# Order of work at the norms of a two-layer hybrid decoder step: first two projections chunk by chunk together, mean squares and roots placed elsewhere

## The chip, the cores and the metric

The kernel runs on one core of a Trainium2 chip. The metric is the device time of one execution in microseconds (us), here the median of three runs. Time is also given inside the profiled execution: its span is the time from the first to the last instruction, and all positions such as "at 38.41" are microseconds from the start of that span.

## The reference, cut to what matters

The program is one step of a small decoder with two layers, for 1024 prompt tokens and 8 sample tokens, 1032 tokens with 1024 features each, in float32. Layer 0 has a mixer of retention and gated delta net heads, layer 1 one of Mamba-2 heads; after each mixer comes a SwiGLU block. Around them stand five RMS norms:

```
def rmsnorm(x, w):
    xf = x.astype(jnp.float32)
    y = xf * lax.rsqrt(jnp.mean(xf * xf, axis=-1, keepdims=True) + EPS)
    return (y * w.astype(jnp.float32)).astype(x.dtype)

for i in range(DEPTH):                       # DEPTH = 2
    h = rmsnorm(x, norm_mix_w[i])
    out, ... = hybrid_mixer(h, ...) if i % 2 == 0 else ssm_mixer(h, ...)
    x = x + out
    x = x + swiglu(rmsnorm(x, norm_ffn_w[i]), ...)
y = rmsnorm(x, norm_final_w)
```

In the kernel they are numbered: norm 0 stands before the mixer of layer 0, norm 1 before its SwiGLU, norm 2 before the mixer of layer 1, norm 3 before its SwiGLU, norm 4 at the end. The states that the mixers also return are left out here, since the change doesn't touch them.

## The kernel before

**Layout.** `x` is kept transposed: 128 partitions hold the features of one of KC = 8 chunks (index c), the free dimension holds the T = 1032 tokens, cut into TG = 3 groups of TN = 344 (index g). TensorE multiplies in a float32 format with fewer bits, so each operand is split into a high and a low part (`h_hi`, `h_lo`, `w_hi`, `w_lo`), and each product is three matmuls: high by high, low by high, high by low. In `group_products` (line 569) that is for one chunk and one group, 128x128 weights against 344 columns.

**Weights** come as units of 128x1024 (all eight chunks of one output tile). SP loads a unit into one of two slots of `w_raw`, GpSimd makes `w_hi` (line 492) and `w_lo` (line 495) of it and counts `w_split` up. GpSimd starts on unit u only when `unit_done` says that TensorE has finished unit u - 2, and SP reloads a slot of `w_raw` when it has been split.

**The results** of projections go to two sets of PSUM banks, `ps_set[0]` and `ps_set[1]`. Jobs take them in turn: `take` waits until whoever read the job before the last in the same set has counted it free. Small results, the mean squares among them, go in the same way to `ps_core[0]` and `ps_core[1]`.

**A norm** is called a boundary; each engine has a function `boundary(n, ...)` that writes out its own order, and the engines meet by semaphores with named steps. There is no planner: program order on each engine is all.

- ScalarE `squares(g)`: two squares of four chunks each (128x1376). For group g it waits until the sum of group g - 1 is made, since they share a buffer.
- VectorE `sums(g)`: two additions (lines 1697 and 1699) that leave 128x688.
- TensorE `mean_square(g)` (line 585): four recorded matmuls with a matrix of ones.
- ScalarE `root(g)`: Ln from `ps_core`, then Exp with -0.5. Each of the two has a table load in front of it.
- VectorE `scaled(g)`: for each chunk one multiplication h = x * weight * root (line 1718) into one of three rotating buffers `h_block`; ScalarE `highs(g)` copies it to `h_hi`; VectorE's `low` (line 1704) makes `h_lo`. Low c - 2 comes behind h c, and h c waits for low c - 3.
- TensorE `projections(g)`: the first two projections of the next stage (`first`: q and k at norm 0, the first gate and up tiles at norms 1 and 3, the scalars and x0 at norm 2), for group g, each chunk waiting for `lo{c}.{g}`. All chunks of the first projection come before those of the second.

Norms 0, 2 and 4 go this way. At norms 1 and 3 the root is not multiplied into h: ScalarE writes `h_hi` as x times the weight (`products`), VectorE `h_lo` (`lows`, line 1729), and the root of all three groups (`logs`, then one Exp) is used behind the projections. So there TensorE need not wait for mean squares, only whoever reads the root.

In front of norms 1, 2 and 3 stand the last outputs of the stage before (`outputs_of(g)`, also line 574 by the record), which VectorE adds to `x` (`add(g, q)`: line 1780 in norms 1, 2 and 4, lines 1811 and 1815 in norm 3). Norm 0 has no outputs: `x` comes by DMA from SP, group by group, and ScalarE's `later_constants` issues four DMAs behind its first squares.

The orders before, g standing for the group:

- TensorE, norms 1 and 3: outputs 0, 1, 2; projections 0; mean square 0; projections 1; mean square 1; projections 2 with mean square 2 between its two.
- TensorE, norms 0, 2, 4: outputs 0, 1; mean square 0; outputs 2; mean square 1; projections 0; mean square 2; projections 1; projections 2.
- ScalarE, norms 0, 2, 4: squares 0, squares 1, root 0, squares 2, highs 0, root 1, highs 1, root 2, highs 2.
- VectorE, norms 0, 2, 4: adds mixed with sums 0 and sums 1, scaled 0, sums 2, scaled 1, scaled 2.

Of the kernel before, what the change touches and what calls it, by code (L numbers as in the profile page):

```python
# [24 lines left out]
KC = D // P  # L25
NP_TOK, ND_TOK = 1024, 8
T = NP_TOK + ND_TOK
TG = 3
# [151 lines left out]
def build(nc, a, o, book):  # L180

    ctx = ExitStack()
    with ctx:
# [364 lines left out]
        def _(pe):  # L548
# [29 lines left out]
            def boundary(n, outputs_of, first):  # L578
# [9 lines left out]

                def projections(g, between=lambda: None):
                    for k, (jobs, job, unit) in enumerate(first):  # L590
                        if k:
                            between()
                        if g == 0:
                            take(jobs, job)
                            pe.wait_ge(w_split, unit + 1)
                        for c in range(KC):
                            pe.wait_ge(*norm_dve[n].value(f"lo{c}.{g}"))
                            mm = group_products(ps_set[jobs.part(job)][:, g, :], unit % 2, c, (h_hi[:, c, :], h_lo[:, c, :]), g,
                                                c == 0, c == KC - 1)
                        if g == TG - 1:  # L600
                            mm.then_inc(unit_done, 1)

                if n in (1, 3):
                    for g in range(TG):
                        outputs_of(g)
                    projections(0)
                    mean_square(0)
                    projections(1)
                    mean_square(1)
                    projections(2, lambda: mean_square(2))  # L610
# [5 lines left out]
                mean_square(1)  # L616
                projections(0)
                mean_square(2)
                projections(1)
# [509 lines left out]
        def _(act):  # L1129
# [20 lines left out]
            def boundary(n):  # L1150
# [29 lines left out]
                def highs(g):  # L1180
                    for c in range(KC if n < 4 else 0):
# [28 lines left out]
                if n == 0:  # L1210
                    later_constants()
                    act.wait_ge(consts_in, 48)
                squares(1)
                root(0)
                squares(2)
                highs(0)
                root(1)
                highs(1)
                root(2)
# [469 lines left out]
        def _(dve):  # L1689
            v = nc.vector  # L1690

            def boundary(n, add):
# [14 lines left out]
                def scaled(g):  # L1707
                    dve.wait_ge(*norm_act[n].value(f"rstd{g}"))
                    for c in range(KC):
# [12 lines left out]
                    if n < 4:  # L1722
# [38 lines left out]
                if n == 0:  # L1761
                    dve.wait_ge(consts_in, 48)
                adds(0, 0)
# [6 lines left out]
                adds(2, 1)  # L1770
                scaled(0)
                sums(2)
                scaled(1)
# [812 lines left out]
```

## Time and profile before

| | |
|---|---|
| median of 3 runs | 3323.36 us (3321.98 to 3327.50) |
| span of the profiled execution | 3317.2 us |
| mean granted TensorE clock | 0.986 |
| TensorE busy | 3143.7 us, 95% |
| VectorE busy | 1775.8 us, 54% |
| GpSimd busy | 1019.1 us, 31% |
| ScalarE busy | 799.8 us, 24% |

The profiled execution has no time of its own beside its span; the three runs stand 4.8 to 10.3 us above the span, which holds only what lies between the first and the last instruction. In the rows below PE is TensorE, PEld its weight loads, DVE VectorE, ACT ScalarE, POOL GpSimd, SP SyncE. A helper records all of ScalarE's operations as line 1131, so there the tiles tell which is which: `work<-ps_core,small` is Ln, `work<-work` of 128x344 is Exp, `work<-x` a square, `h_hi<-work` a high part. The stretches of the norms in the span are: norm 0 from 0 to 62, norm 1 from 885 to 934, norm 2 from 1648 to 1709, norm 3 from 2478 to 2567, norm 4 from 3276 to the end.

### The profile page before, as it was taken

The page shows a single profiled execution, that of the slowest core. Times are in us where ns is not written, and L with a number is a line of the kernel's source. Part 1 is how long each engine was busy: PE and PEld are TensorE (multiplying, and loading weights), DVE is VectorE, ACT ScalarE, POOL GpSimd, SP SyncE. Part 2 cuts the span into 40 slices and gives each one's busy share as a digit, 9 for nine tenths or more (in the row PEclk, how much of TensorE's full clock was granted, in tenths as well). Part 3 has the DMA queues.
Part 4 walks back from the last instruction along what each step waited for, and adds up shares of the span by engine and source line. Part 5 has one row for each costly group of instructions (what it writes and reads, how often), then busy time and mean ns, then how long its engine had stood idle before and what let it go on. Part 6 is the DMA issues. An engine that isn't in the chain of part 4 may idle for free. (4 is left out here: it accounts for less than half of the span.)

```text
span 3317.2 us, 46817 instructions
## 1 busy us (share of the span) xinstructions
PE 3143.7 (95%) x20090; PEld 3030.1 (91%) x20090; DVE 1775.8 (54%) x2023; ACT 799.8 (24%) x1176; POOL 1019.1 (31%) x528
## 2 busy tenths in 40 slices
PE   6999899998899999999989998999988999999997
PEld 5899898888799999999988897989978999999997
DVE  5344657566543333333487869678696333333335
ACT  4222414324420000000145415243253000000002
POOL 2222201111023333333334536345362333333331
PEclk9999999999899999999999999999999999999999
DMA  4111100101011111111113214132231111111111
GB/s 147 59 71 59 49 26 33 40 26 40 21 44 45 50 46 45 45 51 45 45 42 121 86 58 148 62 118 74 82 128 37 51 45 45 50 47 45 46 51 64
DMA packets 94474, 198.15 MB, mean 60 GB/s; under 512 B 21796, under 2 KB 52164, under 8 KB 94152
## 3 DMA queue, kind: packets, MB, share of 16 engines
q1 hardware_dynamic: 52384, 150.03, 12.9%
q10 hardware_dynamic: 41896, 45.23, 4.3%
q8 instruction: 159, 2.61, 0.3%
q14 instruction: 35, 0.29, 0.0%
HBM read 171.41 MB, written 19.59 MB: 58 GB/s over the span
## 5 line engine op out<-in xcount | busy, mean ns | idle before, releaser
L492 POOL CAST w_hi<-w_raw 128x1024 fp32r<-128x1024 f32 x230 | 256.8, 1116 | 2181.2 <-PE ps_set L565 1971.5
L565 PE MATMUL ps_set<-h_hi,w_hi 128*128 128x344 f32 x3648 | 806.0, 329 | 2.2 <-DVE work L2179 1.3
L565 PE MATMUL ps_set<-h_lo,w_hi 128*128 128x344 f32 x3648 | 776.8, 321 | 0.0
L565 PE MATMUL ps_set<-h_hi,w_lo 128*128 128x344 f32 x3648 | 772.0, 320 | 0.0
L565 PEld LDWEIGHTS ps_set<-h_hi,w_hi 128*128 128x128 f32 x3648 | 615.5, 189 | 26.8 <-issue 18.7
L565 PEld LDWEIGHTS ps_set<-h_lo,w_hi 128*128 128x128 f32 x3648 | 619.9, 190 | 0.0
L565 PEld LDWEIGHTS ps_set<-h_hi,w_lo 128*128 128x128 f32 x3648 | 610.6, 188 | 0.0
L495 POOL TENSOR_TENSOR w_lo<-w_raw,w_hi 128x1024 fp32r<-128x1024 f32 x230 | 599.0, 2605 | 18.4
L1824 DVE TENSOR_TENSOR x<-x,ps_set 128x1032 f32<-128x1032 f32 x160 | 196.7, 1229 | 255.6 <-PE ps_set L565 255.6
L1131 ACT ACTIVATE work<-work 128x1032 f32<-128x1032 f32 (+5 forms) x190 | 180.7, 959 | 496.0 <-DVE work L2179 447.9
L565 PE MATMUL ps_set<-y_hi,w_hi 128*128 128x344 f32 x1296 | 282.7, 327 | 8.5 <-DVE y_lo L2360 7.0
L1131 ACT ACTIVATE y_hi<-work 128x1032 fp32r<-128x1032 f32 (+1 forms) x98 | 63.5, 662 | 882.9 <-PE ps_set L565 633.3
L565 PE MATMUL ps_set<-y_lo,w_hi 128*128 128x344 f32 x1296 | 274.6, 320 | 0.0
L565 PE MATMUL ps_set<-y_hi,w_lo 128*128 128x344 f32 x1296 | 273.9, 319 | 0.0
L2179 DVE TENSOR_TENSOR work<-work,ps_set 128x1032 f32<-128x1032 f32 x44 | 54.1, 1229 | 340.4 <-PE ps_set L565 324.0
L565 PEld LDWEIGHTS ps_set<-y_hi,w_hi 128*128 128x128 f32 x1296 | 216.0, 189 | 13.4 <-issue 11.3
L565 PEld LDWEIGHTS ps_set<-y_lo,w_hi 128*128 128x128 f32 x1296 | 218.0, 189 | 0.0
L565 PEld LDWEIGHTS ps_set<-y_hi,w_lo 128*128 128x128 f32 x1296 | 216.5, 189 | 0.0
L836 PEld LDWEIGHTS ps_core<-work 128*128 128x128 f32 x1344 | 159.0, 194 | 29.0 <-issue 8.8
L836 PE MATMUL ps_core<-work 128*128 128x128 f32 x1344 | 169.0, 283 | 16.9 <-DVE work L2071 7.9
L1131 ACT ACTIVATE work<-ps_core 128x512 f32<-128x512 f32 (+3 forms) x164 | 72.9, 451 | 433.5 <-PE ps_core L836 140.2
L1131 ACT ACTIVATE work<-ps_set 128x1032 f32<-128x1032 f32 x72 | 74.3, 1032 | 289.1 <-PE ps_set L565 260.7
(229 smaller groups left out, 3652.7 us busy)
## 6 DMA issues: line engine op xcount, KB each, us to landing
w_raw<-in_w SPq DMA_DIRECT2D x230, 512.0 KB, 3.2
work<-ssm_cum_rows ACTq DMA_DIRECT2D x32, 512.0 KB, 4.8
sample<-in_ssm_state SPq DMA_DIRECT2D x16, 512.0 KB, 5.1
out_ssm_s<-sample SPq DMA_DIRECT2D x16, 512.0 KB, 2.8
x<-in_x SPq DMA_DIRECT2D x6, 688.0 KB, 15.5
work<-work ACTq DMA_DIRECT2D x16, 258.0 KB, 2.4
out_y<-x SPq DMA_DIRECT2D x6, 688.0 KB, 3.4
sample<-bc_rows SPq DMA_DIRECT2D x8, 512.0 KB, 4.7
```

The lines of the kernel that those rows point to most:

```text
L492: return nc.gpsimd.tensor_copy(w_hi[:, k, :], w_raw[:, k, :])
L495: return nc.gpsimd.tensor_tensor(w_lo[:, k, :], w_raw[:, k, :], w_hi[:, k, :].bitcast(F32), ALU.subtract)
L565: mm = nc.tensor.matmul(out[:, g, 0:TN], w[:, slot, cols], v[:, g * TN:(g + 1) * TN], start=(start and n == 0), stop=(stop and n == 2))
L836: mm = nc.tensor.matmul(ps_core[part][:, c * P:(c + 1) * P], blk(lhs)[:, 4 * hf + c], blk(rhs)[:, 4 * hf + c], start=True, stop=True)
L1131: return nc.scalar.activation(out, in_, func, **kw)
L1824: v.tensor_tensor(grp(x[:, t, :]), grp(x[:, t, :]), big(jobs.part(job)), ALU.add).then_inc(jobs.sem(job), 1)
L2179: v.tensor_tensor(grp(tok(c)), grp(RSTD), big(jobs.part(name)), ALU.mult).then_inc(jobs.sem(name), 1)
```

## The change

TensorE gets `together(g)`: for each chunk the products of both projections, one after the other, with a place for other work behind chunk 3. At group 0 it takes both PSUM sets and waits for both weight units ahead of the first product. At norms 1 and 3 it is used for groups 0 and 1; at norm 3 mean square 0 moves behind group 1's products, and mean squares 1 and 2 between the two projections of group 2. At norm 0 mean square 1 moves behind chunk 3 of group 0 and mean square 2 behind chunk 3 of group 1; at norm 2 mean square 2 moves behind chunk 3 of group 0. Group 2 keeps one projection after the other.

ScalarE and VectorE are reordered at norms 0 and 2 alone. At norm 0 root 0 comes ahead of squares 1, and squares, sums and roots of the later groups come in the middle of `highs` and `scaled` of the group before. At norm 2 squares 2 move ahead of most of highs 0, and roots 1 and 2 become Ln, Ln, Exp, Exp, between highs 5 and highs 6 of group 0. Norm 4 keeps its order on all engines.

```
--- before.py
+++ after.py
@@ -586,37 +586,60 @@
                                               start=(k == 0), stop=(k == 1))
                     mm.then_inc(*norm_pe[n].step(f"ms{g}"))
 
+                def product(jobs, job, unit, c, g):
+                    return group_products(ps_set[jobs.part(job)][:, g, :], unit % 2, c, (h_hi[:, c, :], h_lo[:, c, :]), g,
+                                          c == 0, c == KC - 1)
+
+                def together(g, between=lambda: None):
+
+                    if g == 0:
+                        for jobs, job, unit in first:
+                            take(jobs, job)
+                            pe.wait_ge(w_split, unit + 1)
+                    for c in range(KC if first else 0):
+                        pe.wait_ge(*norm_dve[n].value(f"lo{c}.{g}"))
+                        for jobs, job, unit in first:
+                            product(jobs, job, unit, c, g)
+                        if c == 3:
+                            between()
+                    if not first:
+                        between()
+
                 def projections(g, between=lambda: None):
                     for k, (jobs, job, unit) in enumerate(first):
                         if k:
                             between()
-                        if g == 0:
-                            take(jobs, job)
-                            pe.wait_ge(w_split, unit + 1)
                         for c in range(KC):
                             pe.wait_ge(*norm_dve[n].value(f"lo{c}.{g}"))
-                            mm = group_products(ps_set[jobs.part(job)][:, g, :], unit % 2, c, (h_hi[:, c, :], h_lo[:, c, :]), g,
-                                                c == 0, c == KC - 1)
-                        if g == TG - 1:
-                            mm.then_inc(unit_done, 1)
+                            mm = product(jobs, job, unit, c, g)
+                        mm.then_inc(unit_done, 1)
 
                 if n in (1, 3):
                     for g in range(TG):
                         outputs_of(g)
-                    projections(0)
-                    mean_square(0)
-                    projections(1)
-                    mean_square(1)
-                    projections(2, lambda: mean_square(2))
+                    together(0)
+                    if n == 1:
+                        mean_square(0)
+                    together(1)
+                    mean_square(1 if n == 1 else 0)
+
+                    def rest():
+                        if n == 3:
+                            mean_square(1)
+                        mean_square(2)
+                    projections(2, rest)
                     return
                 outputs_of(0)
                 outputs_of(1)
                 mean_square(0)
                 outputs_of(2)
-                mean_square(1)
-                projections(0)
-                mean_square(2)
-                projections(1)
+                if n == 2:
+                    mean_square(1)
+                    together(0, lambda: mean_square(2))
+                    together(1)
+                else:
+                    together(0, lambda: mean_square(1))
+                    together(1, lambda: mean_square(2))
                 projections(2)
 
             def pair_outputs(jobs, job, turn, slot, blocks, rhs, g, done):
@@ -1177,8 +1200,8 @@
                     fn(rstd_of(n, g), ps_core[core.part(f"ms{g}")][:, 0:TN], ACT.Ln, scale=1.0 / D, bias=EPS_C)\
                         .then_inc(core.sem(f"ms{g}"), 1)
 
-                def highs(g):
-                    for c in range(KC if n < 4 else 0):
+                def highs(g, first=0, last=KC):
+                    for c in range(first, last if n < 4 else 0):
                         act.wait_ge(*norm_dve[n].value(f"h{c}.{g}"))
                         fn(h_hi[:, c, span(g)], h_block(n, c), ACT.Copy).then_inc(*norm_act[n].step(f"hi{c}.{g}"))
 
@@ -1210,13 +1233,35 @@
                 if n == 0:
                     later_constants()
                     act.wait_ge(consts_in, 48)
+                    root(0)
+                    highs(0, 0, 4)
+                    squares(1)
+                    highs(0, 4, 6)
+                    root(1)
+                    highs(0, 6)
+                    highs(1, 0, 4)
+                    squares(2)
+                    highs(1, 4, 6)
+                    root(2)
+                    highs(1, 6)
+                    highs(2)
+                    return
                 squares(1)
                 root(0)
+                highs(0, 0, 2)
                 squares(2)
-                highs(0)
-                root(1)
+                if n == 4:
+                    root(1)
+                    root(2)
+                    return
+                highs(0, 2, 6)
+                logs(1)
+                logs(2)
+                for g in (1, 2):
+                    act.wait_ge(*core.read(f"ms{g}"))
+                    fn(rstd_of(n, g), rstd_of(n, g), ACT.Exp, scale=-0.5).then_inc(*norm_act[n].step(f"rstd{g}"))
+                highs(0, 6)
                 highs(1)
-                root(2)
                 highs(2)
 
             def scalars(layer, unit):
@@ -1704,9 +1749,10 @@
                     v.tensor_tensor(h_lo[:, c, span(g)], h_block(n, c), h_hi[:, c, span(g)].bitcast(F32), ALU.subtract)\
                         .then_inc(*norm_dve[n].step(f"lo{c}.{g}"))
 
-                def scaled(g):
-                    dve.wait_ge(*norm_act[n].value(f"rstd{g}"))
-                    for c in range(KC):
+                def scaled(g, first=0, last=KC):
+                    if first == 0:
+                        dve.wait_ge(*norm_act[n].value(f"rstd{g}"))
+                    for c in range(first, last):
                         if n == 4:
                             v.scalar_tensor_tensor(x[:, c, span(g)], x[:, c, span(g)], NORM_W[:, n, c:c + 1], rstd_of(n, g),
                                                    ALU.mult, ALU.mult).then_inc(*end_dve.step(f"y{g}.{c}"))
@@ -1719,7 +1765,7 @@
                                                ALU.mult, ALU.mult).then_inc(*norm_dve[n].step(f"h{c}.{g}"))
                         if c >= 2:
                             low(g, c - 2)
-                    if n < 4:
+                    if n < 4 and last == KC:
                         low(g, KC - 2)
                         low(g, KC - 1)
 
@@ -1759,7 +1805,16 @@
                     return
 
                 if n == 0:
+                    sums(0)
                     dve.wait_ge(consts_in, 48)
+                    scaled(0, 0, 4)
+                    sums(1)
+                    scaled(0, 4)
+                    scaled(1, 0, 4)
+                    sums(2)
+                    scaled(1, 4)
+                    scaled(2)
+                    return
                 adds(0, 0)
                 adds(0, 1)
                 adds(1, 0)
@@ -1767,9 +1822,19 @@
                 adds(1, 1)
                 adds(2, 0)
                 sums(1)
-                adds(2, 1)
-                scaled(0)
+                if n == 4:
+                    adds(2, 1)
+                    scaled(0)
+                    sums(2)
+                    scaled(1)
+                    scaled(2)
+                    return
+                add(2, 2)
+                scaled(0, 0, 2)
+                add(2, 3)
+                scaled(0, 2, 4)
                 sums(2)
+                scaled(0, 4)
                 scaled(1)
                 scaled(2)
```

## Rows read from the trace of the kernel before

**Rows 1.** The page: span and busy time of each engine.
```profile
span 3317.2 us, 46817 instructions
PE 3143.7 (95%) x20090; PEld 3030.1 (91%) x20090; DVE 1775.8 (54%) x2023; ACT 799.8 (24%) x1176; POOL 1019.1 (31%) x528
```
**Rows 2.** Stretches: length, busy by engine, granted clock, DMA share, GB/s.
```profile
0.00:62.00 62.00, 34.69 (x156) 27.10 (x156) 33.86 (x58) 32.43 (x44) 12.21 (x10) 1.00 0.46 162
...
1648.00:1709.00 61.00, 51.46 (x279) 45.40 (x280) 44.91 (x69) 34.51 (x47) 12.45 (x7) 0.94 0.08 26
```
**Rows 3.** Timeline of TensorE, norm 0: start, length, instruction, idle before.
```profile
16.03 2.63 PE L585 MATMUL ps_core<-work,square 128*128 128x344 f32 x4 [16.03 <-DVE work L1699]
```
**Rows 4.** Timeline of ScalarE, norm 0.
```profile
21.00 1.35 ACT L1131 ACTIVATE work<-x 128x1376 f32<-128x1376 f32 x1 [2.88 <-DMA x<-in_x]
22.36 1.28 ACT L1131 ACT_TABLE_LOAD   x1
23.66 0.55 ACT L1131 ACTIVATE work<-ps_core,small 128x344 f32<-128x344 f32 x1
...
25.52 0.49 ACT L1131 ACTIVATE work<-work 128x344 f32<-128x344 f32 x1
```
**Rows 5.** Timeline of VectorE, norm 0.
```profile
22.38 1.59 DVE L1697 TENSOR_TENSOR work<-work 128x1376 f32<-128x1376 f32 x1 [6.49 <-ACT work L1131]
24.01 0.87 DVE L1699 TENSOR_TENSOR work<-work 128x688 f32<-128x688 f32 x1
26.04 1.55 DVE L1718 SCALAR_TENSOR_TENSOR work<-x,small,work 128x344 f32<-128x344 f32 x3 [1.16 <-ACT work L1131]
...
38.41 1.55 DVE L1718 SCALAR_TENSOR_TENSOR work<-x,small,work 128x344 f32<-128x344 f32 x3 [0.53 <-ACT work L1131]
...
49.38 1.55 DVE L1718 SCALAR_TENSOR_TENSOR work<-x,small,work 128x344 f32<-128x344 f32 x3 [2.94 <-ACT work L1131]
...
56.04 1.36 DVE L1704 TENSOR_TENSOR h_lo<-work,h_hi 128x344 fp32r<-128x344 f32 x3
```
**Rows 6.** The chain of work that ended last, norm 3: start, length, work.
```profile
2557.37 3.77 PE ps_set L574 x24
2561.14 1.17 PE ps_core L585 x4
```
**Rows 7.** Stretches of TensorE alone: length, busy, granted clock, DMA share, GB/s.
```profile
909.80:915.10 5.30, 5.27 (x18) 0.50 0.27 99
2531.60:2533.90 2.30, 0.00 (x0) 1.00 0.49 167
2547.00:2550.40 3.40, 3.40 (x14) 0.51 0.00 0
```
**Rows 8.** Timeline of GpSimd, norm 1.
```profile
906.90 2.51 POOL L495 TENSOR_TENSOR w_lo<-w_raw,w_hi 128x1024 fp32r<-128x1024 f32 x1
```
**Rows 9.** Timeline of TensorE, norm 1.
```profile
907.33 0.39 PE L574 MATMUL ps_set<-h_hi,w_hi 128*128 128x344 f32 x1 [1.69 <-DVE h_lo L1729]
...
909.83 0.65 PE L574 MATMUL ps_set<-h_hi,w_hi 128*128 128x344 f32 x1 [1.79 <-DVE h_lo L1729]
```
**Rows 10.** Timeline of VectorE, norm 2.
```profile
1670.65 1.64 DVE L1780 TENSOR_TENSOR x<-x,ps_set 128x688 f32<-128x688 f32 x2
1672.21 3.20 DVE L1718 SCALAR_TENSOR_TENSOR work<-x,small,work 128x344 f32<-128x344 f32 x3
...
1684.83 1.55 DVE L1718 SCALAR_TENSOR_TENSOR work<-x,small,work 128x344 f32<-128x344 f32 x3 [0.53 <-ACT work L1131]
...
1702.46 1.37 DVE L1704 TENSOR_TENSOR h_lo<-work,h_hi 128x344 fp32r<-128x344 f32 x3
```
**Rows 11.** Timeline of GpSimd, norm 2.
```profile
1671.71 2.36 POOL L495 TENSOR_TENSOR w_lo<-w_raw,w_hi 128x1024 fp32r<-128x1024 f32 x1
```
**Rows 12.** Timeline of TensorE, norm 3.
```profile
2538.62 0.43 PE L574 MATMUL ps_set<-h_hi,w_hi 128*128 128x344 f32 x1 [0.64 <-DVE work L1811]
...
2545.73 1.48 PE L585 MATMUL ps_core<-work,square 128*128 128x344 f32 x4 [3.08 <-DVE work L1699]
```

## The prediction

> **What bounds the kernel now.** First the busy shares of the page: TensorE is busy 95% of the span, the next engine in line with work of its own 54% [rows 1]. Between the norms TensorE hardly stops, so the change can only move time inside the norms. The busy time by stretch comes next: in the first 62 us TensorE is busy 34.7, in the 61 us around norm 2 51.5 [rows 2]. These two are bound by the chain square, sum, mean square, root, scaled, high part, low part, which VectorE and ScalarE share. Norms 1 and 3 multiply before the root is known, and there TensorE sets the length but for a few waits. So I read the timelines of the four norms, engine by engine, and lay the new order out with the old durations: each engine takes its instructions in program order and starts one when its last input is there.
>
> The unit prices. A root is Ln 0.55, table load 1.28, Exp 0.49, 2.35 us with the gaps; its first load runs while it waits [rows 4]. Two squares are 2.70 [rows 4], the two sums 2.50 (22.38 to 24.88) [rows 5]. Scaling eight chunks takes 8.02 (49.38 to 57.40, the end of the last three low parts): h0 to h2 in 1.5, then 1.04 for each pair of scaled and low, 1.36 for the last three lows [rows 5]. TensorE does eight chunks of one projection for one group in 3.77 and a mean square in 1.17 [rows 6]; one chunk is 0.47, of both projections 0.94. At half rate a mean square is 2.63 [rows 3] and 18 matmuls take 5.3 us at a granted clock of 0.50, that is 1.2 GHz [rows 7]: 0.88 a chunk, 1.75 for both.
>
> **Norm 0: +8.0.** Removed: the root of group 0 no longer waits behind the squares of group 1, whose x lands at 21.00 [rows 4]. Its mean square ends at 18.66 [rows 3], so the root is there at 18.69 + 2.35 = 21.04 instead of 26.01: 5.0 us early. ScalarE's four loads of constants stay ahead of it and SP's queue is untouched. Added: squares and sums of the next group stand inside the scaling, and its mean square stands behind the products of chunk 3.
> - h0 to h3 and two low parts, 21.07 to 24.15; high 3 ends 24.2; squares of group 1 to 26.95, in which VectorE has nothing to do; sums to 29.45.
> - Only then h4, low 2 (30.4), h5, low 3 (31.5). TensorE has done chunks 0 and 1 from 23.1 and stands still; chunks 2 and 3 at half rate take it to 34.0, the mean square to 35.5 (36.6 if all at half rate).
> - Behind that mean square ScalarE has high 6 and 7 queued, and VectorE behind those low 6, low 7 and all of group 1. Root to 37.9, two high and low parts 1.5: group 1 starts at 39.5. Before it was 38.41 [rows 5]: the 5.0 us are gone and 1.1 lost.
> - Group 1 to group 2, the same loop: first four h and two lows 3.2, squares 2.7, sums 2.5, h4 to low 3 2.05, products 0.94 to 1.75, mean square 1.17 to 2.63, root 2.37, last two high and low 1.5: 16.4 to 18.7. Before: 49.38 - 38.41 = 10.97 [rows 5]. Loss 5.5 to 7.7; as TensorE stands still for 5 us between chunks 1 and 2, I take half rate for part of it, 6.9.
> - Group 2 and the tail (its chunk 7, then the second projection) are as before.
> Sum 1.1 + 6.9 = 8.0; bounds 6.6 (full rate as soon as possible) and 9.6 (half rate to the end of both waits, chunk 2 too). Nothing later hides it: the next projection follows at once.
>
> **Norm 1: +0.1.** Taking both projections at group 0 adds a wait for the second weights, which GpSimd splits after the last output: its low part ends at 909.41 [rows 8]. Queued behind that wait is all of TensorE. Today TensorE does one chunk at 907.33 and then waits until 909.83 anyway [rows 9]: VectorE's second low part is held while GpSimd works. New: start at 909.5 with 16 chunks to do, not 15 from 909.83: 0.47 - 0.33 = +0.1. After it no wait is left on TensorE in either order. Bounds: -1.0, if the half-rate stretch of 5.3 us becomes 3.4 as in norm 3 [rows 7]; +0.4, if it lasts a little longer.
>
> **Norm 2: +1.5.** Group 2's squares go ahead, and the roots of groups 1 and 2 are grouped, Ln, Ln, Exp, Exp: two table loads fewer (2.6 us). But group 1's root now comes only after group 2's mean square, and that stands behind chunk 3 of group 0.
> - From 1670.65 [rows 10] VectorE does add 2, h0, h1 (one of them held to the end of GpSimd's low part, 1674.07 [rows 11], at the latest 1675.0), add 3, h2, low 0, h3, low 1 to 1677.1. Adds read PSUM and took their normal 1.64 for two beside GpSimd's cast; three h beside its low part took 3.20, not 1.55 [rows 5, 10]. Squares of group 2 to 1676.1 (1678.6 if add 3 comes behind a held h1), sums to 1679.6 (1681.1).
> - Low 3 at 1681.6, chunk 3 to 1682.6, mean square to 1683.7; ScalarE's Ln, table, Exp, Exp to 1686.6, high 6 and 7, low 7 at 1688.1. Group 1 starts at 1688.15, before 1684.83 [rows 10]: +3.3.
> - Before, group 2 waited for its root: 1684.83 to the last low at 1703.83 [rows 10]. New, both roots are there: 8.02 + 0.05 + 8.02 = 16.1, end 1704.25: +0.4. With add 3 late 1.6 more, with chunks and mean square at half rate 2.0 more. Bounds +0.4 and +4.0; I take 1.5, nearer the first, since adds were not held in the rows.
>
> On table loads: the trace has one before Ln and one before Exp, each 1.28, with the ACTIVATE 0.02 behind [rows 4]. The Trainium skill (ScalarE: Activation LUTs, What ACT_TABLE_LOAD costs, and Table sets) puts a switch at about 2.66 us with its drain, and says that Ln then Exp needs one load. By the first norm 2 would save 5.3, not 2.6, and come out at -1.2; by the second grouping saves one load at most and norm 2 costs 1.3 more. The rows bear out neither.
>
> **Norm 3: +0.8.** Today the second projection starts at 2538.62, when VectorE has read the bank of output 3; the first, 3.77 us, is done in that wait [rows 6, 12]. Together both wait for 2538.6, and the 3.77 come behind it. Removed: the 3.08 us stop at the mean square of group 0 [rows 12], and the half-rate stretch after it (14 matmuls in 3.4 us [rows 7], 1.7 lost). New: 2538.6 + 6 x 3.77 + 3 x 1.17 = 2564.7 at full rate. But TensorE stands still from the last output at 2531.6 [rows 7] to 2538.6; a stop of 3.1 us brought half rate, so I add up to half of norm 1's 5.3: 2567.3. Before, these products ended at 2557.37 + 3.77 + 1.17 + 3.77 = 2566.1 [rows 6]. Bounds -1.4 and +1.2; by the clock I take +0.8. The final root keeps its place 3.8 us ahead of TensorE's end.
>
> **Norm 4 and the rest: 0.** Its splits are empty or joined. Alternating two banks every three matmuls, which these rows don't price: 0, with under 1 us in all as its bound, since weights are loaded before each matmul either way. The last group of each norm still goes one projection after the other, so weights are released as before.
>
> **Sum:** 8.0 + 0.1 + 1.5 + 0.8 = +10.4 us on the span of 3317.2 [rows 1]. The median of the runs is 3323.36, 6.2 more, which lies outside the first and last instruction and which the change leaves alone: 3323.36 + 10.4 = 3333.8.
>
> **Rivals.** A measurement of this kernel can tell about 0.2%, 6.6 us, from no change.
> - *The early start carries (not slower), 0.10.* If the root of group 1 were there when high 6 is due (32.1), norm 0 would run at VectorE's pace: 21.07, 8.02 for each group and 5.2 twice for squares and sums end the last low at 55.5, not 57.4: -1.9. With -1.0, +0.4 and -1.4 in the others -3.9: 3319.5; half of this case may pass 0.2%. It needs the mean square at 29.7. For it: x is landed and VectorE idle. Against: the sums end at 29.45 and chunk 2's low part at 30.4.
> - *The clock pays for it (within 0.2%), 0.15.* Full rate after all new stops: 6.6 - 1.0 + 0.4 - 1.4 = +4.6: 3328.0. Half rate after a stop of 3.1 us speaks against it [rows 7, 12].
> - *Half rate in every new gap (slower), 0.20.* 9.6 + 0.4 + 4.0 + 1.2 = +15.2: 3338.6. For it: the new stops are 4 to 7 us long.
> - *My sum, 0.55,* with a range of its own of 3329 to 3338.
> Faster 0.05, same 0.05 + 0.15 = 0.20, slower 0.75. The range that leaves out 2 in 10: 3326 to 3340.
>
> **What would show it.** Norm 0: first root at 21.0; VectorE idle from 24 to 27; TensorE still for 4 to 5 us between chunks 1 and 2; group 1's first scaled chunk at 39 to 41, group 2's at 56 to 59; first projections end at 69 to 71, not 62. Norm 2: two table loads fewer, group 1 about 3 us later behind sum 1, last low 0 to 4 later. Norm 3: first products 7 us behind the last output, no stop at the mean square. I am wrong if group 2 of norm 0 starts before 53, or if a stretch between norms changes its length by over 1 us.

## The result, and the profile after

The changed kernel takes 3339.25 us (median of 5 executions, 3338.16 to 3340.60), beside 3326.11 (3321.98 to 3331.18) of the kernel before on the same chip. The ratio is 1.0042 with an interval of 1.0029 to 1.0054: 14 us slower, 10 to 18. Forecast were +10.4 and 3333.8. The sign was right, and the time lies at the upper end of the range of 3326 to 3340, but above the 3329 to 3338 that the prediction gave its own sum. The interval of 10 to 18 holds 10.4, so the total alone can't tell how good the terms are. The stages can: two of the four terms are about 2 us too small.

The page of the changed kernel answers to [rows 1]:
```profile
span 3337.8 us, 46816 instructions
PE 3152.7 (94%) x20090; PEld 3043.6 (91%) x20090; DVE 1773.7 (53%) x2023; ACT 795.4 (24%) x1174; POOL 1017.3 (30%) x528
```
Two instructions fewer on ScalarE are the two table loads of norm 2. The spans differ by 20.6 us, which is more than the times do. Two profiled executions are not two kernels, so I cut each profile into stages at the same instructions. E0 to E3 are the ends of the first two projections of norms 0 to 3. M is the start of the last mean squares inside the gated-delta layer, ahead of norm 1. S is the start of the last mean squares inside the SSM layer, ahead of norm 3.

| us, from the timelines | to E0 | E0 to M | M to E1 | E1 to E2 | E2 to S | S to E3 |
|---|---|---|---|---|---|---|
| before | 62.05 | 820.40 | 55.76 | 770.27 | 779.89 | 77.71 |
| after | 72.05 | 823.34 | 56.05 | 771.30 | 784.94 | 79.04 |
| difference | +10.0 | +2.9 | +0.3 | +1.0 | +5.0 | +1.3 |

From E3 to the end both take 751.1. Forecast were +8.0, 0, +0.1, +1.5, 0, +0.8. The four norms give 12.6. The other 8.0 are in two long stretches that the change does not touch.

**Norm 0**, the same stretches as [rows 2], length and busy time by engine:
```profile
0.00:62.00 62.00, 28.03 (x111) 23.25 (x111) 28.67 (x48) 28.62 (x39) 8.77 (x8) 0.97 0.43 153
1648.00:1709.00 61.00, 50.61 (x285) 47.50 (x284) 44.11 (x55) 24.72 (x35) 13.62 (x7) 0.92 0.10 35
```
In the first 62 us TensorE does 111 matmuls, where it did 156. ScalarE's timeline (start, length, instruction, idle before):
```profile
19.05 1.28 ACT L1154 ACT_TABLE_LOAD   x1 [8.23 <-PE ps_core L585]
20.35 0.55 ACT L1154 ACTIVATE work<-ps_core,small 128x344 f32<-128x344 f32 x1
...
22.21 0.49 ACT L1154 ACTIVATE work<-work 128x344 f32<-128x344 f32 x1
...
33.00 1.28 ACT L1154 ACT_TABLE_LOAD   x1
37.76 0.55 ACT L1154 ACTIVATE work<-ps_core,small 128x344 f32<-128x344 f32 x1 [3.47 <-PE ps_core L585]
...
55.56 0.55 ACT L1154 ACTIVATE work<-ps_core,small 128x344 f32<-128x344 f32 x1 [2.52 <-PE ps_core L585]
```
The first root ends at 22.70, not at 21.04: its table load starts only when the mean square is there. That of the second root runs at 33.00, long before its mean square. VectorE's timeline answers to [rows 5]:
```profile
28.43 1.59 DVE L1742 TENSOR_TENSOR work<-work 128x1376 f32<-128x1376 f32 x1 [2.61 <-ACT work L1154]
...
40.52 0.94 DVE L1749 TENSOR_TENSOR h_lo<-work,h_hi 128x344 fp32r<-128x344 f32 x2 [5.55 <-ACT h_hi L1154]
41.57 1.55 DVE L1764 SCALAR_TENSOR_TENSOR work<-x,small,work 128x344 f32<-128x344 f32 x3
...
58.32 0.94 DVE L1749 TENSOR_TENSOR h_lo<-work,h_hi 128x344 fp32r<-128x344 f32 x2 [4.60 <-ACT h_hi L1154]
59.37 1.55 DVE L1764 SCALAR_TENSOR_TENSOR work<-x,small,work 128x344 f32<-128x344 f32 x3
...
66.03 1.36 DVE L1749 TENSOR_TENSOR h_lo<-work,h_hi 128x344 fp32r<-128x344 f32 x3
```
The idle times are the two waits foreseen: 2.61 for squares of the next group, 5.55 and 4.60 in which it stands, with its own inputs ready, behind ScalarE's queued root. Group 1 starts at 41.57 (it was 38.41), group 2 at 59.37 (49.38). TensorE, with stops where [rows 3] had its first wait:
```profile
16.34 2.63 PE L585 MATMUL ps_core<-work,square 128*128 128x344 f32 x4 [16.34 <-DVE work L1744]
...
31.91 0.66 PE L574 MATMUL ps_set<-h_hi,w_hi 128*128 128x344 f32 x1 [3.20 <-DVE h_lo L1749]
...
50.66 0.43 PE L574 MATMUL ps_set<-h_hi,w_hi 128*128 128x344 f32 x1 [4.82 <-DVE h_lo L1749]
```

**Norms 1 and 3** on TensorE, answering to [rows 9, 12]:
```profile
922.52 0.62 PE L574 MATMUL ps_set<-h_hi,w_hi 128*128 128x344 f32 x1 [4.00 <-POOL w_lo L495]
...
2558.02 0.63 PE L574 MATMUL ps_set<-h_hi,w_hi 128*128 128x344 f32 x1 [7.19 <-DVE work L1876]
```
The last number is the wait ahead of the first product of both projections: 4.00 us for the second weights, 7.19 us for the PSUM bank. Stretches of TensorE alone behind the second one and behind a stop of norm 0 (length, busy, granted clock, DMA share, GB/s):
```profile
2558.00:2561.40 3.40, 3.38 (x12) 0.50 0.02 5
2561.40:2564.80 3.40, 3.40 (x18) 0.74 0.00 0
...
50.60:54.10 3.50, 3.44 (x13) 0.55 0.02 5
```
At full rate 24 matmuls take 3.77 us [rows 6]. Here 12 take 3.38 at a granted clock of 0.50, which is 1.2 GHz. **Norm 2** on ScalarE has Ln, Ln and the two Exps behind one load:
```profile
1696.68 0.55 ACT L1154 ACTIVATE work<-ps_core,small 128x344 f32<-128x344 f32 x1
1697.73 0.55 ACT L1154 ACTIVATE work<-ps_core,small 128x344 f32<-128x344 f32 x1 [0.50 <-PE ps_core L585]
1698.30 1.28 ACT L1154 ACT_TABLE_LOAD   x1
1699.59 0.87 ACT L1154 ACTIVATE work<-work 128x344 f32<-128x344 f32 x2
```

### The profile page after: what moved, and what is told of

It is laid out like the page before. It is cut to its first block and busy times, and to the rows that moved or that the text cites. A ratio compares the mean times of both kernels' runs of the same rounds, so it can differ in the third digit from the quotient of the medians.

```text
span 3337.8 us, 46816 instructions
## 1 busy us (share of the span) xinstructions
PE 3152.7 (94%) x20090; PEld 3043.6 (91%) x20090; DVE 1773.7 (53%) x2023; ACT 795.4 (24%) x1174; POOL 1017.3 (30%) x528
## 3 DMA queue, kind: packets, MB, share of 16 engines
q8 instruction: 159, 2.61, 0.3%
```

## The experiments

All times are medians. A ratio stands to the kernel before on the same chip and has its 95% interval behind it. The stages come from the profile of the run.

**The kernel before, unchanged**, to see how a profile of it differs from another one.

> The kernel before, once more, for a second profile. Theory A (the changed kernel loses at the norms alone; the two stretches between norms that were longer in its profile, 823.3 us against 820.4 from the end of norm 0's products to the last mean squares ahead of norm 1, and 774.2 against 769.4 from the end of norm 2's products to the first outputs ahead of norm 3, differ from one execution to the next): ratio 1.000, and these stretches come out between the two values or near the longer, with a span of 3320 to 3328. Theory B (the change makes these stretches longer, by where it puts what follows): they come out at 820.4 and 769.4 again, within 0.5 us, span 3317.

Measured: 3323.81 against 3322.74, ratio 1.0002 (0.9993 to 1.0011). The span was 3322.8, 5.6 above the first profile of the same program. E0 to M took 820.38, as in the first profile, so this run left open whether the 823.3 of the changed kernel comes from the change. E2 to S took 788.42, where the first profile had 779.89; S to E3 took 76.13 (77.71), M to E1 54.61 (55.76). So the first profile was a short one from E2 to S, and the 5.0 us between it and the changed kernel there prove nothing.

**One norm alone.** Each kernel is the one before with the diff's parts for one norm: all three engines at norms 0 and 2, TensorE alone at 1 and 3. For norm 1:
```diff
-                    projections(0)
+                    together(0)
                     mean_square(0)
-                    projections(1)
+                    together(1)
```

> The kernel before with the new order at norm 0 alone, on all three engines. Theory A: norm 0's products end at 72.0 and not 62.05, +10.0 us, and that is all: +9.5 to +10.5 in time, three quarters of the whole change. Theory B: +10.0 at the norm and some 3 to 8 more in the stretches behind it, +13 to +18 in time. My forecast's sum had +8.0 here.

> The kernel before with the new order at norm 1 alone (TensorE only). From the last mean squares ahead of the norm to the end of its products the order before took 54.5 in three profiles and 55.5 to 55.9 in five. Theory A: the new order takes 54.6 to 56.1, by where the clock falls, since both wait for the same moment, the end of GpSimd's low part: within 0.3 us of before on the mean, nothing in time. Rival: as TensorE stands still without the one chunk, its clock always falls, and the norm takes 56 or more, +1.

> The kernel before with the new order at norm 2 alone. Theory A: +1.0 us, as in the profile of the changed kernel; the first scaled chunk of group 1 some 4 us later behind sum 1, and given back as group 2 doesn't wait for its root: not to be told from no change in time. Theory B: +1 at the norm and some 5 more behind it, from norm 2 to norm 3.

> The kernel before with the new order at norm 3 alone (TensorE only). Theory A: products start 7.2 us behind the last output, no stop at the mean square, half rate for the first 3 to 5 us; +1.0 to +1.6 us at the norm. If the full rate held through the 7 us stop, -1.4.

| | median | before | ratio | its stage | E0 to M | E2 to S |
|---|---|---|---|---|---|---|
| norm 0 | 3331.36 | 3322.74 | 1.0027 (1.0017 to 1.0038) | 71.79 | 820.28 | 781.36 |
| norm 1 | 3323.97 | 3322.81 | 1.0000 (0.9991 to 1.0009) | 56.00 | 823.06 | 785.63 |
| norm 2 | 3322.96 | 3322.74 | 1.0002 (0.9993 to 1.0011) | 771.31 | 820.33 | 781.91 |
| norm 3 | 3325.76 | 3322.74 | 1.0012 (1.0003 to 1.0021) | 78.95 | 821.60 | 781.54 |

The ratios add up to 1.0041, and the whole change measures 1.0042. Each of the four intervals is about 3 us wide either way, so by time alone this says little, but the stages agree: each is as long with its part alone as in the two profiles of the whole change. Norm 0 costs 9.0 us (5.6 to 12.6) in time and 9.7 to 10.0 at its stage. Norm 3 costs 4.0 (1 to 7). Norms 1 and 2 are too small for the time. By the stages norm 2 costs 1.0, the same in all three profiles that have it (771.3 against 770.25). Norm 1 takes 56.0 to 56.1 in three profiles; in the old order it takes 54.5 to 55.9, and about 0.8 less in the mean, so by the whole stage the rival of the expectation had it right. But part of this lies ahead of the norm's first product, where the change does nothing: from M to the end of the last output four of the ten old profiles take 22.2 us, and the other six 23.1 to 23.3, as all three new ones do. From the last output to E1 the old order takes 32.3 to 32.6 and the new one 32.9, so the change costs 0.3 to 0.6, 0.5 in the mean.

At norm 3 the expectation of +1.0 to +1.6 was too small. The stage is 79.0 in all three profiles with the new order. In the eight with the old order and mean square 0 ahead it is 76.1 in six and 77.7 in two. What separates those is TensorE's clock at the old stop. In the second profile of before:
```profile
2552.87 1.39 PE L585 MATMUL ps_core<-work,square 128*128 128x344 f32 x4 [2.62 <-DVE work L1699]
```
and the granted clock behind this stop:
```profile
2552.90:2556.30 3.40, 3.40 (x18) 1.00 0.00 0
2556.30:2559.70 3.40, 3.40 (x24) 1.00 0.00 0
```
The profile that I predicted from had 0.51 there [rows 7], after a stop of 3.08 us. The old order has half rate elsewhere too: behind the wait of 2.4 us ahead of the first projection, where the second profile of the kernel before has 13 matmuls in 3.40 us at a granted clock of 0.56. Seven of the eight profiles with the old order have such a stretch there, and only the one that I predicted from has not (21 matmuls, 1.00). It costs nothing, as TensorE waits for the sum of mean square 0 afterwards in any case. The new order, alone, has a stop and half rate each time:
```profile
2540.07 0.63 PE L574 MATMUL ps_set<-h_hi,w_hi 128*128 128x344 f32 x1 [7.23 <-DVE work L1853]
```
```profile
2540.10:2543.50 3.40, 3.40 (x12) 0.50 0.02 5
2543.50:2546.90 3.40, 3.40 (x19) 0.79 0.00 0
```

**Norm 0, mean square behind chunk 1.** If group 1 waits for a closed loop (mean square behind chunk 3, root behind it, high 6 and 7 behind the root), moving it from behind chunk 3 to behind chunk 1 must bring every later group forward, by 2.4 and 6.0 us.
```diff
-                    together(0, lambda: mean_square(1), 3)
-                    together(1, lambda: mean_square(2), 3)
+                    together(0, lambda: mean_square(1), 1)
+                    together(1, lambda: mean_square(2), 1)
```
The last argument is the chunk behind which the mean square stands.

> The kernel before with the new order at norm 0 alone, but each mean square behind the products of chunk 1 and not of chunk 3. Theory A (the loss at norm 0 is the closed loop: the mean square waits for the products of chunk 3, those for low 3, that for the sums, and high 6 and 7 for the root): group 1 starts 2.4 us earlier than with chunk 3, group 2 6.0 us earlier, since then the table load behind high 5 and not the mean square comes last; norm 0's products end at 65.8 (71.8 with chunk 3, 61.9 before), and the time is +2.5 to +4 over before. Theory C (the loss is the squares and sums inside the scaling, wherever the mean square stands): the products still end at 70 or later, time +8.

Measured: 3326.19 against 3324.72, 1.0012 (1.0003 to 1.0021); E0 at 65.63. TensorE, and VectorE's first scaled chunks of groups 1 and 2:
```profile
30.62 1.79 PE L585 MATMUL ps_core<-work,square 128*128 128x344 f32 x4 [2.40 <-DVE work L1749]
...
45.93 2.63 PE L585 MATMUL ps_core<-work,square 128*128 128x344 f32 x4 [4.00 <-DVE work L1749]
```
```profile
37.65 1.55 DVE L1769 SCALAR_TENSOR_TENSOR work<-x,small,work 128x344 f32<-128x344 f32 x3
...
52.96 1.55 DVE L1769 SCALAR_TENSOR_TENSOR work<-x,small,work 128x344 f32<-128x344 f32 x3
```
The same two of norm 0 alone:
```profile
40.09 1.55 DVE L1769 SCALAR_TENSOR_TENSOR work<-x,small,work 128x344 f32<-128x344 f32 x3
...
59.10 1.55 DVE L1769 SCALAR_TENSOR_TENSOR work<-x,small,work 128x344 f32<-128x344 f32 x3
```
Group 1 is 2.44 earlier and group 2 is 6.14 earlier. These two lines take back 6.2 of the 9.8 us, as laid out beforehand, and so the loop is shown. Between these two kernels the squares, sums and scaling on VectorE and ScalarE are the same, so it is the place of the mean square, not the squares inside the scaling, that costs most.

**The same with the constants' wait ahead.** ScalarE then has only one wait between its first squares and the root.
```diff
-                    later_constants()
                     act.wait_ge(consts_in, 48)
+                    later_constants()
                     root(0)
```

> The new order at norm 0 with the mean squares behind chunk 1, and ScalarE's wait for the constants ahead of its four DMAs and not directly ahead of the wait for the first mean square. In the profiles the table load ahead of the first root stood behind that wait (it began 0.08 us after the mean square ended), other roots have it done while they wait. Theory: two waits in a row hold the load back; apart, it runs ahead, the first root is there at 21.0 and not 22.3, and the norm's products end at 64.3 and not 65.6. Rival: the load waits for the mean square for another reason; then nothing changes.

ScalarE's timeline:
```profile
11.27 1.28 ACT L1168 ACT_TABLE_LOAD   x1 [0.79 <-issue]
...
18.67 0.55 ACT L1168 ACTIVATE work<-ps_core,small 128x344 f32<-128x344 f32 x1 [6.12 <-PE ps_core L585]
```
The load is out of the wait; Ln follows the mean square at once. E0 comes at 64.42, 1.2 earlier. The time, 3327.22 against 3322.81, 1.0014 (1.0005 to 1.0023), can't tell 1.2 us.

**Norm 0 with TensorE kept busy** in its two stops, by matmuls of constants into PSUM columns that nothing else uses; the rest is norm 0 alone.
```diff
+                def keep_busy(n_):
+                    for _ in range(n_):
+                        nc.tensor.matmul(ps_set[0][:, 2, 344:472], ones, ident, start=True, stop=True)
...
+                        if n == 0 and c == 1:
+                            keep_busy((5, 10)[g])
```

> The new order at norm 0 alone, with idle work for TensorE (5 and 10 small matmuls into unused PSUM columns behind chunk 1 of groups 0 and 1; the result isn't used), so that its clock doesn't fall in the new stops. If half rate has the share that I gave it (1.0 us in the first loop, 1.4 to 2.1 in the second), the products of chunks 2 and 3 of group 1 take 1.9 us and not 3.6 to 3.8, the mean square 1.3 and not 1.3 to 2.5, and the norm's products end 2 to 3 us earlier, at 69 to 70. If the clock plays no part, at 71.8 or later.

Behind the two stops, norm 0 alone and then this kernel:
```profile
31.56:34.90 3.34, 3.34 (x12) 0.54 0.00 0
49.10:52.90 3.80, 3.71 (x13) 0.50 0.02 4
```
```profile
31.42:33.50 2.08, 2.08 (x12) 1.00 0.00 0
47.70:49.90 2.20, 2.12 (x13) 1.00 0.00 0
```
Twelve matmuls take 2.08 us in place of 3.34, and E0 comes at 67.71 instead of 71.79: half rate was 4.1 of norm 0's 9.8 us. The prediction had counted some 2.4 of it, and the expectation 2 to 3. The time does not show this (3330.40 against 3324.72, 1.0027, 1.0015 to 1.0038). The profile of this run took 823.04 from E0 to M, where norm 0 alone took 820.28, so part of the gain is lost there in this execution; whether that holds for all of them is open, and that norm 0 gets faster in time by it is not shown.

**Norm 3 with TensorE kept busy** ahead of the first product, otherwise norm 3 alone.
```diff
+                    keep_busy(20)
                     together(0)
```

> The new order at norm 3 alone, with 20 small idle matmuls (into unused PSUM columns) in the 7 us between the last output and the first product. If half rate has its share, the first products no longer run at half rate, and the 96 matmuls of groups 0 and 1 take 15.1 us and not 17.5; the norm gets 2.4 us shorter than with the new order alone, about 0.5 us longer than before, where it was 2.9 longer. If not, 2.9 longer still. Should the idle matmuls last beyond 7 us, the start moves by what is over.

TensorE, and its clock behind the start:
```profile
2540.52 4.63 PE L605 MATMUL ps_set<-square 128*128 128x128 f32 x40
...
2547.88 0.40 PE L574 MATMUL ps_set<-h_hi,w_hi 128*128 128x344 f32 x1 [2.73 <-DVE h_lo L1776]
```
```profile
2547.90:2551.30 3.40, 3.40 (x22) 1.00 0.00 0
2551.30:2554.70 3.40, 3.40 (x23) 1.00 0.00 0
```
The stage falls from 78.95 to 76.72, and the time stands at 3323.89 against 3324.72, 0.9999 (0.9990 to 1.0007). So of norm 3's 2.8 us over the usual 76.13, the clock is 2.2 and the wait itself the other 0.6, close to the 2.4 and 0.5 expected.

**Norm 3 in the old order, mean square 0 later.** The first projection keeps its place in the wait for the bank; only the mean square, whose sum comes late, goes behind group 1.
```diff
                     projections(0)
-                    mean_square(0)
                     projections(1)
-                    mean_square(1)
-                    projections(2, lambda: mean_square(2))
+                    mean_square(0)
+                    projections(2, lambda: (mean_square(1), mean_square(2)))
```

> The kernel before with one edit at norm 3: the mean square of group 0 stands behind the products of group 1, and those of groups 1 and 2 between the two projections of group 2, as in the new order, but groups 0 and 1 keep one projection after the other. Theory A (norm 3 loses because the first projection of group 0 no longer runs while VectorE reads the last bank, and gains by the stop that goes): without the first and with the second the norm gets shorter than before by 2.6 to 3.1 us, the stop at the mean square, and by up to 1.6 more where a half-rate stretch followed it; time -2.5 to -4. Theory D (the stop at the mean square was no loss, as something else ends the norm): no change.

Measured: 3319.19 against 3324.72, 0.9989 (0.9980 to 0.9998), 3.7 us faster (0.7 to 6.6); the stage takes 73.39, 2.7 less than 76.13. The view of waits for TensorE from 2536 to 2565 has a single row (waited for, total, times, longest), and the timeline shows where:
```profile
PE ps_set L574 <- DVE work L1853: 2.4, 1, 2.4
```
```profile
2536.98 0.65 PE L574 MATMUL ps_set<-h_hi,w_hi 128*128 128x344 f32 x1 [2.38 <-DVE work L1853]
```
It has the part of the change that moves mean squares at norm 3, and not the part that takes the projections together. It differs from the kernel with norm 3 alone in nothing but that, so by the stages (78.95 and 73.39) taking them together costs 5.6 us, and moving the mean squares gains 2.7.

**The same, and at norm 1 too** mean square 0 behind group 1.
```diff
                     projections(0)
-                    mean_square(0)
                     projections(1)
+                    mean_square(0)
                     mean_square(1)
```

> The kernel before with the mean square of group 0 behind the products of group 1 at norms 1 and 3, one projection after the other everywhere. Norm 3 as with that edit alone, 73.4 us and not 76.1; at norm 1 the mean square of group 0 stopped TensorE for 0.45 us where its clock had not fallen before, and not at all otherwise: -0 to -0.4. Time -3 to -4.

Norm 3's stage was 73.45 again, norm 1's 55.67, as in the old order: nothing to win at norm 1, where TensorE waits for no mean square. The time was 3322.03 against 3322.81, 0.9996 (0.9987 to 1.0005). Expected were 3 to 4 us less; this is 1.3 less, with an interval from 4.3 less to 1.7 more. So the stage of norm 3 is shorter by 2.7 in both runs, and in time the gain stands in one of them only.

**The changed kernel again**, for the two long stretches.

> The changed kernel once more, for a second profile. Theory A (losses at the norms alone: 10.0, some 1, 1.0 and 2.9 us; 823.3 us from norm 0 to the last mean squares ahead of norm 1, and 784.9 from norm 2's products to the mean squares ahead of norm 3, are scatter): norm lengths as in the first profile within 0.5 us, the first stretch at 820.4, 821.6 or 823.3, the second anywhere from 780 to 788; ratio 1.0040 to 1.0045. Theory B: 823.3 and 784.9 again.

Measured: 3338.75 against 3322.81, 1.0043 (1.0029 to 1.0057). Its stages: 71.62, 823.20, 56.13, 771.28, 785.20, 78.96. The two long stretches came out as theory B had them, 823.20 and 785.20. But norm 1 alone, which is the kernel before up to that point, has 823.06 as well from E0 to M, so the change isn't needed for it. From E2 to S the same kernel, whose norms 2 and 3 are in the old order, has 785.63. And the stages of the four norms add up to 14.2 (9.9, 0.5, 1.0 and 2.8 over the usual old length), where the time says 14 (10 to 18), so what the long stretches add in the mean can't be told from nothing. From E0 to M the difference is a clock that falls in the middle of the stage. Windows of 20 us, from 380 us behind E0, for after, before and norm 1 alone:
```profile
452.00:472.00 20.00, 19.93 (x137) 0.91 0.00 1
```
```profile
442.00:462.00 20.00, 19.86 (x148) 1.00 0.00 1
```
```profile
442.00:462.00 20.00, 19.93 (x136) 0.91 0.00 1
```
Over all 14 profiles E0 to M is 820.3 to 823.3 and E2 to S 779.9 to 788.4, old and new orders mixed. At norm 2's part, E1 to E2, and from E3 on, nothing of the sort is seen (770.24 to 770.27 in the eleven profiles with the old norm 2). Why TensorE falls to half rate between E0 and M in one execution and not in the next stays open, and so does what makes E2 to S differ.

## What the prediction had right, and which steps failed

**Sign and mechanism: right; two terms failed.** The change was to cost time at norm 0, for one root that comes early and two that come late, and a little at norms 2 and 3. The runs with one norm each show that. The steps that failed are "the root is there at 18.69 + 2.35" at norm 0, whose term of 8.0 measured 9.9, and "Removed: ... the half-rate stretch after it" at norm 3, whose term of 0.8 measured 2.8 over the usual length. Norms 0, 1 and 3 all lie above the upper bounds that the prediction gave them (9.6, 0.4 and 1.2), and norm 2 is 0.5 below its term. That the total still fell into the wide range is owed to its width, and not to the terms.

**"Norm 0: +8.0": mechanism right, size 10.0.** The losses by VectorE's timeline: 3.2 to the start of group 1 (forecast 1.1), 6.8 from group 1 to group 2 (17.80 now, 10.97 before; forecast 6.9), 0.0 behind it. The first term failed at the step "the root is there at 18.69 + 2.35". It took the table load as already done and cites [rows 4] for a load that runs during a wait. They show no such thing: that load, at 22.36, comes straight behind the squares, when the mean square had long been there (18.66). Here, ahead of the root stood two waits in a row, for constants and for the mean square, and the load stayed behind the second: 1.3 us, shown by moving the wait (1.2 at E0). Another 0.3 is a mean square that ends at 18.97 and not at 18.66, since `x` landed later in this execution. The last 0.4 is what is left of the next mean square, 2.21 us behind half-rate products and not 1.5, as the steps around it came out 0.3 shorter. That the second term fits is luck: with norm 0 alone the first loop loses less (group 1 at 40.09) and the second 8.0 (59.10 - 40.09 = 19.0), with nearly the same end. Half rate falls more into the one loop or more into the other, and keeping TensorE busy in both stops showed what it takes in all, 4.1 us.

**"Norm 1: +0.1": 0.3 between the two profiles, 0.5 in the mean from the last output on.** The start was as laid out, one wait for the low weights. What I missed is that the clock behind the old wait differs from one profile to the next, and that I read one of the slower ones. In the second profile of before the clock behind the same wait is 0.69 and 0.74, where [rows 7] have 0.50:
```profile
908.00:911.00 3.00, 2.26 (x9) 0.69 0.50 153
911.00:914.00 3.00, 3.00 (x16) 0.74 0.06 22
```
Behind the new stop of 4.0 us 18 or 19 products ran at half rate each time, and E1 came 32.9 after the last output.

**"Norm 2: +1.5": 1.0.** Group 1 starts 3.9 us later than in the kernel before if each is counted from its own E1 (forecast 3.3), and the last low part ends 1.0 later (forecast 0.4, and 1.1 for a late add or half rate). Both are 0.6 past the floor of the prediction, so once group 1 starts the rest runs at VectorE's pace, as laid out. Add 3 did come behind a held h1, and most of the 1.6 us put on that did not show at the end. Two loads went, and the two roots' Exps are 0.87 together.

**"Norm 3: +0.8": 1.3 between the profiles, 2.5 in the mean of the eight, 2.8 over the usual length.** Under "Removed" I counted two things: the 3.08 us stop, rightly, and 1.7 us of half rate behind it. That second one was there in two of eight profiles of the old order. What I added for the new half-rate stretch held at its full price (12 matmuls in 3.38 us, then 18 in 3.40): counted from S, its 2567.3 is 78.9, and the stage measured 79.0. I then took 0.4 off "by the clock", for which nothing spoke. So the step that failed is "Removed: ... the half-rate stretch after it": a loss of one execution was booked as a loss of the kernel.

**"Norm 4 and the rest: 0": right.** Stages without a norm change by up to 3 and 8 us from execution to execution, under any order. My own condition for being wrong, a stretch between norms that changes by over 1 us, was met and meant nothing: the second profile of before, against the first, meets it too.

**The rivals.** The early start did not carry. The clock did not pay: the long stops of norms 0 and 3 brought half rate, and norm 1 ended late. "Half rate in every new gap", 3338.6, is nearest to the time; it was right in sign at norms 0, 1 and 3, too small at 3, and wrong at norm 2 (1.0, not 4.0). I gave it 0.20 for its 15.2 us. Stops of 4 to 7 us against one of 3.1 with half rate behind it should have earned it more.

## What to carry to other kernels

When work of the next group is put inside the current one, follow the loop to its end: a mean square behind chunk 3 delayed the high parts that chunks 6 and 7 need, and moving it two chunks forward gave back 6 of 10 us. Let the engine that is the bound do what is ready, even one projection of two, while it waits for the second: taking them together at norm 3 turned 3.77 us of cover into a stop, and the stop into half rate, 5.6 us in all. Take one profile's clock state as one draw, and compare stages cut at the same instructions over several profiles before a microsecond is booked to an edit.

## What the runs showed of the hardware that I had not expected

- A table load on ScalarE ran ahead of one wait (it started at 11.27, its Ln at 18.67) but not ahead of two in a row (it started at 19.05, 0.08 behind the mean square's end). The difference was 1.2 us at E0.
- At the same place of the same order, ahead of mean square 0 of norm 3, a stop of TensorE of 2.45 to 2.62 us was followed by full rate in six profiles, and one of 2.65 and one of 3.08 by half rate. But the wait of 2.4 us ahead of the first projection there was followed by half rate in seven of the same eight, so the length of the stop does not settle it. The stop of 7.2 us was followed by half rate and a stage of 79.0 in each of three profiles. Matmuls of constants in the stop kept the clock at 1.00.
- Behind the first stop of norm 0 (31.91, 3.20 us) the record of the clock says 1.00, but the twelve products stand 0.29 us apart and the mean square takes 2.21, as at 0.50 elsewhere; 0.16 apart is full rate. So the durations are to be read with the clock:
```profile
32.36 0.49 PE L574 MATMUL ps_set<-h_lo,w_hi 128*128 128x344 f32 x1
32.65 0.49 PE L574 MATMUL ps_set<-h_hi,w_lo 128*128 128x344 f32 x1
...
35.51 2.21 PE L585 MATMUL ps_core<-work,square 128*128 128x344 f32 x4
```
- While GpSimd made a low weight part, VectorE operations on SBUF alone took longer: at norm 2 two h took 3.14 us beside it, and a sum of 128x688 2.93 in place of 0.87. Adds that read PSUM did not: in the kernel before the one of 128x688 that ran beside a low part took 0.86, and the 40 of 128x1032 took 1.23, as elsewhere.
